# Turning scan tables on VectorE in the conv stage, and four-group tiles in the states stage

## The reference, cut to what matters

```python
A_bar = jnp.exp(A * dt)
B_bar = ((A_bar - 1.0) / A)[..., None] * Bm
bu = jnp.einsum("gnp,blgp->blgn", B_bar, u)
_, h = lax.associative_scan(s5_combine, (a, bu), reverse=reverse, axis=1)
return jnp.einsum("gpn,blgn->blgp", Cm, h).real
# y = forward + backward + s5_d * u, then gelu, GLU, and a gated sum with the conv branch
```

## Time and profile before

| | value |
|---|---|
| median of 3 runs | 2432.13 us (2431.12 to 2433.3) |
| the profiled execution | 2434.09 us |
| its span | 2432.4 us |
| TensorE clock granted | 0.998 |
| `s5a` on TensorE | 433.14 to 485.75 us |

### The profile page before, as it was taken

One profiled execution on the slowest core, in us unless ns is written; L12 is line 12 of the kernel. 1 busy time (PEld: TensorE's weight loads), 2 busy tenths in 40 slices (PEclk: granted clock), 3 DMA queues, 4 the chain that ended last, 5 costly groups with the idle time before them and its releaser, 6 DMA issues.

```text
span 2432.4 us, 34372 instructions
## 1 busy us (share of the span) xinstructions
PE 2403.5 (99%) x12524; PEld 2184.9 (90%) x12524; DVE 1643.0 (68%) x3028; ACT 771.5 (32%) x1277; POOL 255.3 (10%) x263
## 2 busy tenths in 40 slices
PE   8999999999999999999999999999999999999998
PEld 6788888788889788888889999999999999999997
DVE  7735553578883884262474687888888788777776
ACT  6401110322223331130252253433333343332333
POOL 0088850000000220000000000001001000000000
PEclk9999999999999999999999999999999999999999
DMA  7532227632127542213332122233233622222222
GB/s 250 166 125 94 82 74 150 187 126 86 72 79 218 201 186 79 95 51 122 115 111 87 44 71 68 83 102 106 92 103 101 257 78 68 76 77 83 76 76 76
DMA packets 121663, 267.25 MB, mean 110 GB/s; under 512 B 15553, under 2 KB 67265, under 8 KB 121537
## 3 DMA queue, kind: packets, MB, share of 16 engines
q1 hardware_dynamic: 113552, 239.85, 30.7%
q0 software_dynamic: 6688, 22.55, 2.5%
q10 hardware_dynamic: 1296, 3.17, 0.4%
HBM read 200.55 MB, written 67.08 MB: 110 GB/s over the span
## 4 chain that ended last, share of the span: by engine, by line
PE 93%; DVE 3%; ACT 1%; issue 1%; DMA 1%; SPq 0%; DVEq 0%; ACTq 0%
PE bank L823 30%; PE bank L824 30%; PE bank L825 30%; PE bank L1069 1%; ACT PB L1577 1%; DVE PT L1834 1%; DVE PB L2318 1%; PE bank L1064 0%; PE bank L1016 0%; DVE ON L1834 0%; DVE smx L2310 0%; PE bank L1023 0%; DMA scratch_KV<-KVS 0%; PE bank L993 0%; ACT ON L1317 0%
## 5 line engine op out<-in xcount | busy, mean ns | idle before, releaser
L823 PE MATMUL bank<-XN,WLO 128*128 128x512 f32 x1200 | 468.3, 390 | 4.2 <-DVE SB L2203 3.4
L825 PE MATMUL bank<-XN,WHI 128*128 128x512 f32 x1200 | 467.1, 389 | 0.0
L824 PE MATMUL bank<-XN,WHI 128*128 128x512 f32 x1200 | 467.1, 389 | 0.0
L823 PE MATMUL bank<-XH,EL 128*128 128x384 f32 x1232 | 412.1, 334 | 0.0
L824 PE MATMUL bank<-XL,EH 128*128 128x384 f32 x1232 | 411.5, 334 | 0.0
L825 PE MATMUL bank<-XH,EH 128*128 128x384 f32 x1232 | 411.5, 334 | 0.0
L823 PEld LDWEIGHTS bank<-XN,WLO 128*128 128x128 f32 x1200 | 225.4, 188 | 52.3 <-DVE WLO L1829 3.8
L825 PEld LDWEIGHTS bank<-XN,WHI 128*128 128x128 f32 x1200 | 225.4, 188 | 46.9
L824 PEld LDWEIGHTS bank<-XN,WHI 128*128 128x128 f32 x1200 | 225.4, 188 | 46.7 <-issue 0.5
L823 PE MATMUL bank<-AF,EL 128*128 128x384 f32 (+2 forms) x704 | 236.6, 336 | 0.5 <-DVE HR L2472 0.3
L825 PE MATMUL bank<-AF,EH 128*128 128x384 f32 (+2 forms) x704 | 235.5, 335 | 0.0
(11 more groups left out here) (295 smaller groups left out, 3752.0 us busy)
## 6 DMA issues: line engine op xcount, KB each, us to landing
RAW<-W_all SPq DMA_DIRECT2D x131, 512.0 KB, 3.5
WR<-W_all SPq DMA_DIRECT2D x92, 512.0 KB, 4.3
scratch_G<-GS SPq DMA_DIRECT2D x16, 768.0 KB, 3.7
scratch_VW<-TB POOLq DMA_DIRECT2D x16, 544.0 KB, 3.4
XS<-xT SPq DMA_DIRECT2D x8, 768.0 KB, 5.9
scratch_CO<-COS SPq DMA_DIRECT2D x8, 768.0 KB, 5.0
COL<-scratch_CO SPq DMA_DIRECT2D x8, 768.0 KB, 4.2
G2L<-scratch_G SPq DMA_DIRECT2D x8, 768.0 KB, 5.7
```

The source lines that it names most:

```text
L823: pe_mm(out, w[1], x[0], start=first, stop=False, skip_group_check=onto)
L824: pe_mm(out, w[0], x[1], start=False, stop=False, skip_group_check=onto)
L825: return pe_mm(out, w[0], x[0], start=False, stop=last, skip_group_check=onto)
```

## The change

- V is no longer stored by POOL. In the conv stage DVE turns each tile's V part of TB in 32 x 32 blocks, one instruction for 128 x 512 floats (`turn`, 16 in all), into a new buffer TV (two of 2 KB a partition). SP stores TV to a new tensor `scratch_VT` with four DMAs for each tile, of 32 partitions, in pieces of 32 floats (`store_turned`, 64 DMAs in all). SP's loads of conv weights are interleaved with them in a written-out order.
- POOL waits, before it overwrites the V part of a TB buffer, for the turn that read it (`rows_free`). For its first two tiles, which follow no turn, it waits on the same semaphore for two of the three memsets of Z (L2028). It stores only the W part, whose rows in `scratch_VW` are laid out by tile, direction and group.
- The states stage has tiles of four groups (8 tiles). VT is loaded ready for use (two DMAs, 2 KB pieces); BBL and WK come in one DMA each. The four transposes (L993), the copy of the bank to VT on ACT, and the waits `v_turned` and `v_staged` go.
- The lags take two matmuls of 128 columns for each group instead of four. Within a tile TensorE makes the lags of both pairs of groups, then the states of both; DVE copies both pairs' lags, then both pairs' backward states.
- For the backward direction WK now begins at entry 0 of the nine that a group has; before, at entry 1. The shapes are the same.
- LL moves by 2 KB, still under COS. SP loads tile 0 during "co"; it loads BBL and WK of tile 1 after the last store of COS half 0 has landed, and VT of tile 1 after that of half 1.

The diff, cut to what the prediction speaks of:

```diff
+TILES = GROUPS // QUAD
...
+    TV = [at(f"TV{b}", kb, [4, QUAD, P // 4]) for b, kb in enumerate((73.5, 90))]
...
+    VT = [at(f"VT{b}", kb, [2, QUAD, P]) for b, kb in enumerate((85, 81))]
+    LL = at("LL", 77, [2, 2, LAGS * GP])
+    WK = [at(f"WK{b}", kb, [2, QUAD, P]) for b, kb in enumerate((89, 73))]
+    BBL = [at("BBL0", 93, [2, QUAD, GP]), keep_under("BBL1", [2, QUAD, GP])]
...
+    W_d = nc.dram_tensor("scratch_VW", (P, TILES, 2, QUAD, NPOW * GP), F32).ap()
+    VT_d = nc.dram_tensor("scratch_VT", (TILES, 2, P // 4, 4 * QUAD, P), F32).ap()
...
+        def store_turned(d, t):
+            sp.wait_ge(S("rows_free"), 2 + TILES * d + t + 1)
+            for k in range(4):
+                sp.dma_start(VT_d[t, bass.ds(d, 1), :, :, 32 * k:32 * (k + 1)].rearrange("o r m c -> (o r) m c"),
+                             TV[t % 2][32 * k:32 * (k + 1)].rearrange("r j g c -> r (j g) c")).then_inc(S(f"turned_stored{t % 2}"), 16)
+        weights(SLOT0["conv"] + 2, 0)
+        with loop(nc.sync, 2) as i:
+            for jj in range(2):
+                s, t = 3 * jj + SLOT0["conv"] + 2, 4 * jj
+                store_turned(i, t)
+                weights(s + 1, (s + 1) % 2, 3 * i)
+                store_turned(i, t + 1)
+                weights(s + 2, s % 2, 3 * i)
+                store_turned(i, t + 2)
+                weights(s + 3, (s + 1) % 2, 3 * i)
+                store_turned(i, t + 3)
...
+                sp.dma_start(VT[par][:, d].rearrange("p g c -> p (g c)"),
+                             VT_d[bass.ds(t, 1), d].rearrange("o r (j g) c -> j (o r) (g c)", j=4)
+                             ).then_inc(S(f"turned_in{par}"), 16)
+        def load_w(t, par):
+            sp.dma_start(BBL[par][:], BB_d[:, :, bass.ds(QUAD * t, QUAD), :].rearrange("d p g c -> p d g c")
+                         ).then_inc(S(f"lag_in{par}"), 16)
+            sp.dma_start(WK[par].rearrange("p d g c -> p (d g) c"),
+                         one_tile(W_d, t)[:, :, :, :, 0:P].rearrange("p o d g c -> p (o d g) c")
+                         ).then_inc(S(f"lag_in{par}"), 16)
...
-                for par in range(2):
-                    load_v(par, par)
-                    load_w(par, par)
+                load_turned(0, 0)
+                load_w(0, 0)
...
+        sp.wait_ge(S("mix_stored0"), 96)
+        load_w(1, 1)
+        sp.wait_ge(S("mix_stored1"), 96)
+        load_turned(1, 1)
...
+                t = 2 * i + par
+                if more:
+                    sp.wait_ge(S("lags"), 2 * t + 2)
+                    load_w(t + 2, par)
+                for h in range(2):
+                    store_lags(2 * t + h, h)
+                if more:
+                    sp.wait_ge(S("states_bwd"), 2 * t + 2)
+                    load_turned(t + 2, par)
...
                     pool.wait_ge(S(f"tables_stored{par}"), 16 * (4 * d + i))
+                    pool.wait_ge(S("rows_free"), TILES * d + 2 * i + par + 1)
...
-                    pool.dma_start(W_d[:, bass.ds(g0, 4), ROW * d:ROW * (d + 1)], TB[:, par]
-                                   ).then_inc(S(f"tables_stored{par}"), 16)
+                    pool.dma_start(W_d[:, bass.ds(2 * i + par, 1), d].rearrange("p o g c -> p (o g) c"),
+                                   TB[:, par, :, C * GP:]).then_inc(S(f"tables_stored{par}"), 16)
...
-                pe.wait_ge(S(f"s5a_in{par}"), 64 * (i + 1))
-                for j in range(4):
-                    last = nc.tensor.transpose(PS[par][:, j * P:(j + 1) * P], VN[:, par, j, :], ident[:])
-                last.then_inc(S("v_turned"), 1)
...
-                    nc.tensor.matmul(out[:, z:z + GP], bb, kb[:, z:], start=True, stop=False)
-                    nc.tensor.matmul(out[:, z:z + GP], bf, kf[:, 0:GP], start=False, stop=True)
-                    nc.tensor.matmul(out[:, 0:z], bb, kb[:, 0:z], start=True, stop=True)
-                    last = nc.tensor.matmul(out[:, z + GP:], bf, kf[:, GP:], start=True, stop=True)
-                last.then_inc(S("lags"), 1)
-                pe.wait_ge(S("v_staged"), it + 1)
...
+                pe.wait_ge(S(f"lag_in{par}"), 32 * (i + 1))
+                for h in range(2):
+                    if not (isinstance(i, int) and i == par == 0):
+                        pe.wait_ge(S("lags_staged"), 2 * t + h - 1)
+                    for g in range(2):
+                        out = PS[6 + h][0:GP, g * LAGS * GP:(g + 1) * LAGS * GP]
+                        bf, bb = (BBL[par][:, d, 2 * h + g] for d in range(2))
+                        kf, kb = (WK[par][:, d, 2 * h + g] for d in range(2))
+                        z = (C - 1) * GP
+                        nc.tensor.matmul(out[:, 0:z + GP], bb, kb, start=True, stop=False, skip_group_check=True)
+                        last = nc.tensor.matmul(out[:, z:], bf, kf, start=False, stop=True, skip_group_check=True)
+                    last.then_inc(S("lags"), 1)
+                pe.wait_ge(S(f"turned_in{par}"), 32 * (i + 1))
+                for h in range(2):
+                    it = 2 * t + h
+                    if not (isinstance(i, int) and i == par == 0):
+                        pe.wait_ge(S("h_fwd"), 4 * (it - 1))
+                        pe.wait_ge(S("h_bwd"), 4 * (it - 1))
+                    elif h == 0:
+                        pe.wait_ge(S("u_in"), 128)
+                        pe.wait_ge(evac, RES0["gate"])
+                    for d, (bank0, made) in enumerate(((2, "states_fwd"), (4, "states_bwd"))):
+                        for g in range(2):
+                            last = nc.tensor.matmul(PS[bank0 + h][:, g * NC:(g + 1) * NC], VT[par][:, d, 2 * h + g, :],
+                                                    one(U, 2 * it + g), start=True, stop=True)
+                        last.then_inc(S(made), 1)
...
-                act.wait_ge(S("v_turned"), it + 1)
-                if not isinstance(i, int):
-                    act.wait_ge(S("states_bwd"), it - 1)
-                copy(VT[:, par, :], PS[par][:]).then_inc(S("v_staged"), 1)
...
+        step.up(V.memset(Z[:, 0:1], 0.0))
+        for col in (T_PROMPT + 1, T + 2):
+            V.memset(Z[:, col:col + 1], 0.0).then_inc(S("rows_free"), 1)
+        dve.wait_ge(S("rows_free"), 2)
         dve.wait_ge(step.sem, step.n)
+        def turn(d, t):
+            dve.wait_ge(S("tables_made"), 2 * TILES * d + 2 * t + 1)
+            dve.wait_ge(S(f"turned_stored{t % 2}"), 64 * (TILES // 2 * d + t // 2))
+            V.transpose(TV[t % 2].rearrange("p j g c -> p g j c"),
+                        TB[:, t % 2, :, 0:C * GP].rearrange("p g (j c) -> p g j c", j=4)
+                        ).then_inc(S("rows_free"), 1)
...
                     V.tensor_tensor(XC[:, zcols(b)], take(q + b, i, each), RB[:, blk(b)], ALU.mult
                                     ).then_inc(evac, 1)
+                    if b != 1:
+                        turn(i, 4 * jj + b // 2)
                 lo(SLOT0["conv"] + 3 * jj + 2, 6 * i)
...
+                    if b == 1:
+                        turn(i, 4 * jj + 2)
...
+                    else:
+                        turn(i, 4 * jj + 3)
...
+            dve.wait_ge(S(f"turned_stored{par}"), TILES * 4 * 16)
...
+            for par in range(2):
+                it = 2 * i + par
                 dve.wait_ge(S("states_bwd"), it + 1)
```

More of the change, by code:

```diff
@@ L441, in _ @@
             sp.dma_start(U_d[j * P:(j + 1) * P], UB[:, j % 2]).then_inc(S(f"mix_stored{j % 2}"), 16)
-        with loop(nc.sync, 6) as i:
-            for par in range(2):
-                weights(SLOT0["conv"] + par + 2, par, i)
+        def store_turned(d, t):
[3 more added lines that the diff above has]
+                             TV[t % 2][32 * k:32 * (k + 1)].rearrange("r j g c -> r (j g) c")).then_inc(S(f"turned_stored{t % 2}"), 16)
@@ L449, in load_v, with load_turned @@
+        def load_turned(t, par):
             for d in range(2):
[L450 to L459, removed]
+                sp.dma_start(VT[par][:, d].rearrange("p g c -> p (g c)"),
+                             VT_d[bass.ds(t, 1), d].rearrange("o r (j g) c -> j (o r) (g c)", j=4)
+                             ).then_inc(S(f"turned_in{par}"), 16)
@@ L463, in _ @@
         for j in range(4):
-            weights(SLOT0["co"] + j + 2, j % 2)
+            if j:
+                weights(SLOT0["co"] + j + 2, j % 2)
             if j == 2:
@@ L467, in _ @@
                     sp.wait_ge(S(f"tables_stored{par}"), 2 * 4 * 16)
+                    sp.wait_ge(S(f"turned_stored{par}"), TILES * 4 * 16)
                 sp.wait_ge(S("bb_stored"), 32)
-                for par in range(2):
-                    load_v(par, par)
-                    load_w(par, par)
+                load_turned(0, 0)
+                load_w(0, 0)
             for e in range(2):
@@ L493, in store_lags, with s5a @@
                          ).then_inc(S(f"lags_stored{par}"), 16)
[L495 to L499, removed]
-            for par in range(2):
[L501 to L504, removed]
+        def s5a(i, more):
```

(16 more changed lines are left out.)

44 lines of the change are left out of this document (3 added, 41 removed).

## The result

| | before | changed |
|---|---|---|
| median of 9 runs (range), us | 2432.21 (2431.12 to 2433.37) | 2437.38 (2437.01 to 2442.87) |
| ratio to before, 95% interval | 1 | 1.0032 (1.0023 to 1.0040) |
| profiled execution, us | 2434.09 | 2442.38 |
| states stage on TensorE in it, us | 433.14 to 485.45, 52.3 | 432.85 to 494.09, 61.2 |

The end of the stage is the start of the first gate product. Before, the timeline has it at 485.45; the 485.75 of the table ahead of the prediction is a later point of the chain.

A forecast was written before the change was run, and what follows sets the result against it. TensorE, busy 99% of the span, was taken as the bound; the states stage, paced by DMAs to 472.5 plus 0.5 us, would gain 12.75 us, conv work costing nothing: 2432.13 - 12.75 = 2419.4 us, range 2416.5 to 2425.5.

The forecast's parts named there:

- And the DMAs: States stage: 9.0 MB after 434.06 at 266 GB/s are in at 470, so TensorE's last states end at 472.5.
- VectorE's 2.20 us an iteration: States stage: lag copy, skip terms and H copies without waits; from 438.34, sixteen iterations end at 473.5, TensorE at 470.4.
- Part 1: States stage, TensorE: the four transposes an iteration go, 0.53 us each iteration, 8.5 us in all.
- Part 2: States stage, TensorE: lags in two matmuls of 128 columns a group instead of four gain 2.1 us over 32 groups.
- Part 3: States stage, TensorE: the wait for the copy to VT goes, worth 1.6 us, ends 0 and 3.2 us.
- The sum for the stage: States stage: latest of three paths 472.5, plus 0.5 us meshing loss, ends at 473.0; gain 12.75 us (8.2 to 15.4).
- (a): Conv stage: 16 turns on VectorE at 1.1 us, 18 us (8 to 35), hidden in its idle time; cost nothing.
- (b): Conv stage: POOL starts 15.5 us later, last store at 360.7, waits at most 4.3 us each; cost nothing, limit 18 us.
- rival 4: Conv stage: turned tables come late through POOL, about no change, 2433 us; chance 0.06, shared with any loss cancelling the gain.
- (c): Conv stage: turned stores, 32768 packets at 27 ns, take 55 us over 16 engines; hidden up to 68 ns a packet.
- rival 3: Conv stage: partial writes above 68 ns a packet choke the queue; at 90 ns 2449 us, slower than before; chance 0.08.
- rival 1: States stage: DMAs pace it at 232 GB/s, TensorE ends at 477.5, gain 8.2 us, 2423.9 us; chance 0.18.

The follow-up runs named there:

- four-load kernel: Changed kernel with a tile's VT loaded by four DMAs of 32 partitions instead of two of outermost dimension 4: 2424.18 us, 0.9965 of the kernel before.
- both edits: Changed kernel with VT loaded by four DMAs of 32 partitions and lag stores issued on ScalarE's queue: 2422.60 us, 0.9962 of the kernel before.

## Why the prediction was wrong

**The step that failed** stands under "And the DMAs": "The VT pieces are four times longer and the BBL pieces twice as long, so I take the upper rate." The rate of 266 GB/s was read off loads spread over the engines and was given to one that uses four. What the runs show in its place is some 87 GB/s while such a load is in flight, 6.0 us for the 512 KB of a tile's VT, and tiles 7.0 to 7.8 us apart in place of 4.5. The rate itself was fair for spread loads: the four-load kernel moved 7.11 MB in 34 us at 77.3%, which is 271 GB/s at a share of 1. I looked at the length of a piece, and not at how many engines would carry it, though the diff shows the 4 in front.

```profile
DMA  9999999961157830599967797596599447669999
GB/s 228 197 320 360 279 230 193 300 184 46 36 159 241 221 78 11 94 270 363 262 207 185 167 305 219 157 277 182 114 223 305 130 133 248 211 127 190 304 346 282
...
q1 hardware_dynamic: 10212, 7.11, 77.3%
```

This is that kernel's DMA view of 440 to 474 us: no flat stretch at a quarter.

**A wait left out.** VectorE's 2.20 us an iteration was right as work, but LL has two halves, and the copy of an iteration waits until the lags of two iterations before have landed. Before, this wait hid in 3.0 us an iteration. At 2.2 us it doesn't, even with spread loads (11.6 us in the four-load kernel). In the changed kernel the two waits feed each other: the chain that ended last goes store of the lags, lag copy, store of the lags, at 5.7 to 5.9 us each.

```profile
465.51 5.72 DMA scratch_L<-LL
471.26 0.66 DVE LL L2133
...
472.82 5.85 DMA scratch_L<-LL
478.69 0.66 DVE LL L2133
```

**Point by point.**
- *Part 1*, 8.5 us for the transposes: they are gone, and TensorE's work of a tile is 4.6 us where 4.5 was forecast. Right as work.
- *Part 2*, 2.1 us: worth some 0.4 us alone in the kernel before, by the trace, since the lags lay beside ScalarE's copy. It counts only with part 3, and the sum, which took both, did not depend on the split.
- *Part 3*: with both edits a tile without a wait takes 4.65 us, of which the states hold TensorE for 455.82 - 453.03 = 2.79 us; forecast were 4.5. So the wait for the copy is gone as the sum had it, and 8 x 0.15 = 1.2 us of TensorE's work were missed.
- *The sum for the stage*, an end at 473.0, against 485.75, which should have been 485.45 (0.3 us less gain): with the loads spread and the lag stores on another queue it is 475.76. So 2.8 us of the miss are the tile's size, 1.2 us, and waits; the other 18.3 us (494.09 - 475.76, one profiled execution each) are what those two edits bring back. By the medians it is 2437.38 - 2422.60 = 14.8 us.
- *(a) the turns*: 16 at 0.70 us, where I took 1.1. They waited 18.6 us for POOL, at most 4.3 at a time as forecast, and TensorE paid nothing: it is busy for 180.00 of the 180 us from 180 to 360, and starts the stage at 432.85, before the old 433.14.
- *(b) POOL's late start*: last store at 364.2, forecast 360.7. That is 19.0 us later than before, past the 18 us that I had called the limit, and still TensorE has no wait of over 0.9 us as it turns to "co" (367.38). So the limit was drawn too tight, and rival 4 did not show.
- *(c) the turned stores*: the queue's share from 180 to 360 us rose from 10.9% to 24.7%, with the 60 x 512 = 30720 packets of the turned stores issued in that stretch: 0.138 x 16 x 180 / 30720 = 13 ns a packet, half of the 27 I took and far under the 68 of rival 3. By the rule of the Trainium skill weighed in the prediction, "DMA: Bandwidth & Descriptors", Specifications, my estimate was about 54 ns; the measurement decides: no such price shows here.

The changed kernel: the group of the turns on VectorE, then POOL's last store, the queue from 180 to 360 us, and that window:

```profile
L2046 DVE STREAM_TRANSPOSE TV<-TB 128x512 f32<-128x512 f32 x16 | 11.3, 704 | 18.6 <-POOL TB L819 18.6
```

```profile
364.17 0.79 POOL L827 DMA_DIRECT2D scratch_VW<-TB  x1 [0.79 <-POOL TB L825]
```

```profile
DMA packets 34848, 15.46 MB, mean 86 GB/s; under 512 B 32158, under 2 KB 32158, under 8 KB 34846
...
q1 hardware_dynamic: 33406, 10.23, 24.7%
```

```profile
180.00:360.00 180.00, 180.00 (x795) 149.05 (x795) 104.16 (x96) 22.96 (x24) 156.61 (x117) 1.00 0.33 86
```

The kernel before, the same queue and stretch:

```profile
DMA packets 4128, 15.44 MB, mean 86 GB/s; under 512 B 480, under 2 KB 480, under 8 KB 4128
...
q1 hardware_dynamic: 1728, 6.29, 10.9%
```

- *The rivals*: rival 1 had the right place and the wrong mechanism. It priced a full queue at 232 GB/s; what came was a queue three quarters empty for long stretches. The sign I had named, TensorE idle for a DMA in the second half of the stage, did show it. The range ended at 2425.5 because its slow end was the rate of a crowded but spread queue; its other end was VectorE's, and neither had a queue in which one load is held to few engines.

**The clock.** From 440 to 480 us the mean granted clock is 0.91 of the 2.4 GHz level, against 1.00 before from 452 to 480. In three tiles, each behind a wait for VT, the states take 4.40 to 4.51 us instead of 2.86. It is no cause of the loss: from the states at 469.72 (slow) to those at 477.12 are 7.40 us, from 462.39 (fast) to 469.72 are 7.33 us. The load sets the pace either way.

**The two groups of times.** They come from the start of "glu", 315 us behind the states stage. There VectorE makes a weight slot's WLO and GpSimd multiplies a tile of gates with the conv branch, at nearly the same moment. In the profiled execution of the changed kernel:

```profile
808.80 3.45 POOL L834 TENSOR_TENSOR G2L<-G2L,COL 128x1536 f32<-128x1536 f32 x1 [443.85 <-DMA G1L<-scratch_G]
...
808.92 4.42 DVE L1839 TENSOR_TENSOR WLO<-WR,WHI 128x1024 fp32r<-128x1024 f32 x1 [1.29 <-ACT WHI L1333]
```

In the kernel with the lag stores on ScalarE's queue, whose states stage ends at nearly the same time (493.80 against 494.09):

```profile
808.07 1.23 DVE L1835 TENSOR_TENSOR WLO<-WR,WHI 128x1024 fp32r<-128x1024 f32 x1 [1.28 <-ACT WHI L1326]
808.17 4.50 POOL L827 TENSOR_TENSOR G2L<-G2L,COL 128x1536 f32<-128x1536 f32 x1 [444.04 <-DMA G1L<-scratch_G]
```

Whoever starts second, here by 0.1 us, takes longer: 4.4 us instead of 1.23 for VectorE, 4.5 instead of 3.45 for GpSimd. TensorE needs that WLO and waits 3.2 us for VectorE in the first case, not at all in the second; behind the wait the granted clock also fell for a while (mean 0.96 from 792 to 831 us, against 1.00).

From the first gate product to the end of the span are 1946.6 us in the first case and 1941.7 in the second: 4.9 us, about the distance of the groups.

In all eleven traces the two go together: GpSimd first in eight, with 4.4 to 4.5 us for WLO and 1944.6 to 1947.9 us behind the stage; VectorE first in three, with 1.23 us and 1941.3 to 1941.7. No trace is of the changed kernel in its lower group, so for its own executions this is inferred. The kernel before went the long way in its profile, and the kernel with both edits the short one, so its profiled 2418.79 us owes some 5.6 us to this and not to the change.

**What stays open.** What decides who is first at the start of "glu"; what part of the 3.2 us between the best kernel and the forecast is the wait for lag stores, and what the slow start of the second tile; and the gain of the transposes alone, with buffers that let the loads run ahead. LL with four halves, which would take VectorE's wait away, was not tried, as it has no room beside the tiles of this stage.

## What to carry to other kernels

Before a rate is given to a load, read its outermost dimension on both sides: by this case it says how many DMA engines carry it, and a rate measured on another load holds only for the same number. In a trace, look for waits on a DMA while the mean share stands flat at a quarter or an eighth, with small transfers landing late. And when a step is taken out, ask what it freed early: the copy to VT cost time, but released the buffer that the next loads needed. Before two medians a few us apart are compared, see whether the executions fall in groups, and whether the profiled ones are of the same group.

## What the hardware showed unexpectedly

- A load whose outermost dimension is 4 holds up all others: with it in flight, 512 KB of WK took 8.6 us to land and a store of 30 KB 5.7 us; with the load spread 4.7 and 3.0 to 3.5 us. With a dimension of 2 it was 10.0 and 8.8 us.
- Writes of 128 bytes cost 13 ns of one DMA engine each; there was room for 68.
- The same instruction of 128 x 1024 on VectorE took 1.23 us when it started 0.1 us ahead of a product of 128 x 1536 on GpSimd, and 4.4 us when it started 0.1 us behind it.
- A turn of 128 x 512 in blocks on VectorE takes 0.70 us, as long as a plain product of that size.
